# Routed experts of a mixture layer in three fp32r products instead of one fp32 product, with two output row buffers and another order of the weight loads

## The chip, the cores and the metric

The kernel runs on one core of a Trainium2 chip. The metric is the time of one execution on the device in microseconds, the median of several runs. A core has five engines with an instruction queue each: TensorE (PE; its weight loads are shown apart as PEld), VectorE (DVE), ScalarE (ACT), GpSimd (POOL) and SyncE (SP, which issues most DMAs). Engines wait for each other and for DMAs through semaphores only. Sixteen DMA engines move the data.

## What is computed

One layer of a transformer for 640 tokens of 1024 elements, with attention in two forms, and behind it a mixture of 64 small experts, of which each token takes eight. The part that the change touches is this:

```python
def swiglu(x, w1, w3, w2):
    return (jax.nn.silu(x @ w1) * (x @ w3)) @ w2

# tokens sorted by expert and padded to blocks of 128 rows; one expert a block
def run_block(args):
    xb, e = args
    return swiglu(xb, w_e1[e], w_e3[e], w_e2[e])      # 128x1024 @ 1024x256 (twice), 128x256 @ 256x1024
yd = lax.map(run_block, (xd.reshape(n_blocks, 128, d), blk_e)).reshape(n_rows, d)
return jax.ops.segment_sum(yd * wd[:, None], td, num_segments=t)
```

All is float32. A token goes to 8 experts, so there are 5120 rows, 80 to a block on average if every expert has one block; experts with more than 128 rows get a second block. With these inputs there are 70 blocks, the last six of them such second blocks with few rows.

## The kernel before

**The stages.** Modulation and norm, projections, two attentions, the merge and output projection (L1088 to L1217, which already works with rounded and remainder parts), router and shared expert, and then the loop over the routed blocks (L1685 to L1889), which takes from 1080 to 1905 us of the profiled execution. A last stage reads the sums back and adds the residual.

**The loop.** Every engine runs its own `step(n, i, u, guard)` for n = 0, 1, 2, ...; u is n modulo RING (4). `run` (L1688) unrolls the first four steps, runs the steps 4 to 63 in a loop of four, and then further fours with conditions on the number of blocks `nb`, which is only known at run time. `due` puts such a condition around a part. One step works on up to four blocks:

- GpSimd (L1744): `gather(n)` copies the block's row numbers and gathers its 128 rows from DRAM to `xg[n % 2]` by an indirect DMA (L1762), then `scatter(n-3)` (L1766) copies row numbers, waits for the scatter before (`s_sc`) and for the scaled output (`yV`, `yA`), and adds the rows of `yb` to the sums in DRAM with an indirect DMA that accumulates (L1777). Scatters of two blocks may hit the same token, so they run one at a time. `hold` (L1750) is a one-element instruction ahead of each.
- TensorE (L1788): `turn_x(n)` transposes the gathered rows (8 transposes, L1794), `down(n-2)` is the second layer (L1806: 4 products of 512 columns), `turn_g(n-1)` transposes the hidden rows (L1813), `up(n)` is the first layer with w1 and w3 side by side (L1821: 8 products of 512 columns). A float32 product is two MATMUL instructions in the profile.
- ScalarE (L1832): its half of `take_x(n)` (L1837, copy out of PSUM), its half of `take_y(n-2)` (L1845, scaled by the routing weight), `silu(n)` (L1853).
- VectorE (L1861): the other halves (L1866, L1873), `take_g(n-1)` (L1878), `product(n)` (L1882).
- SyncE (L1709): w1 and w3 of block n (`load_w13`, L1487, 2 x 1 MB, 8 KB to a partition each) once `up(n-4)` is done, then w2 (`load_w2`, L1491, 1 MB in rows of 4 KB) once `down(n-4)` is done. The weights of blocks 0 to 2 are loaded in the stage before.

There is one `yb`, so `take_y` of a block waits until the scatter of the block before has landed.

## Time and profile before

| | |
|---|---|
| median of 3 runs | 1926.02 us (1924.02 to 1927.55) |
| profiled execution, span | 1923.9 us |
| TensorE busy | 1775.5 us (92%) |
| VectorE, ScalarE, GpSimd busy | 574.9, 375.0, 430.1 us |
| granted TensorE clock, mean | 0.967 of full |
| data moved by DMA | 346 MB, 180 GB/s |
| loop over the routed blocks | 1080 to 1905 us |

Times in the rows are microseconds from the start of the span, or ns where a mean of one instruction is given. A busy time is what an engine worked; what stands after the bar or in brackets is how long it stood before, and for whom. Matmuls overlap in the pipeline: an instruction's own duration is longer than the distance from its start to the next one's, and the distance is what counts.

### The profile page before, as it was taken

Reading aid. Unit: us, or ns where it says so; the run is one execution under the profiler, and the core shown is the slowest. Engines: PE = TensorE matmul, PEld = TensorE weight load, DVE = VectorE, ACT = ScalarE, POOL = GpSimd, SP = SyncE. Lnnn points to the kernel's source line nnn. Section 1 sums busy time; section 2 is a strip of 40 time slices with the busy share of each in tenths; the row PEclk is TensorE's granted clock in tenths of the full one; section 3 lists DMA queues with packets and bytes.
Section 4 is the critical chain, followed back from the end, with each engine's and each line's share of the span. In section 5 each row is a group of like instructions: output and inputs, shape, how many; then the busy total and the mean of one; then the engine's idle time right before and its main releaser. Section 6 shows DMA issues by size and latency. Waiting matters only on the chain. (4 is left out here: it accounts for less than half of the span.)

```text
span 1923.9 us, 21816 instructions
## 1 busy us (share of the span) xinstructions
PE 1775.5 (92%) x7487; PEld 1077.7 (56%) x7487; DVE 574.9 (30%) x1221; ACT 375.0 (19%) x722; POOL 430.1 (22%) x630
## 2 busy tenths in 40 slices
PE   7979999869999799999985799999999999999993
PEld 2457767556666699996452344444444444444441
DVE  2444454454445500211661011121112121112213
ACT  3112222222323411220210111111111111111110
POOL 0010000020011233230016122333223333223321
PEclk9989999989999999999987899999999999999996
DMA  9311212200000332325250499999999999999953
GB/s 329 139 45 44 87 58 73 78 22 1 0 0 0 110 87 66 87 66 192 81 219 13 177 333 340 339 338 323 322 329 341 334 329 314 322 326 324 319 183 111
DMA packets 127327, 346.37 MB, mean 180 GB/s; under 512 B 20698, under 2 KB 60206, under 8 KB 109240
## 3 DMA queue, kind: packets, MB, share of 16 engines
q1 hardware_dynamic: 105130, 301.18, 42.2%
q0 software_dynamic: 21440, 42.08, 9.3%
q10 hardware_dynamic: 720, 2.62, 0.3%
q8 instruction: 22, 0.36, 0.1%
q14 instruction: 15, 0.12, 0.0%
HBM read 332.01 MB, written 45.25 MB: 196 GB/s over the span
## 5 line engine op out<-in xcount | busy, mean ns | idle before, releaser
L1821 PE MATMUL psum<-mem 128*128 128x512 f32 x1120 | 495.5, 595 | 1.1 <-DVE mem L1866 1.1
L1821 PEld LDWEIGHTS psum<-mem 128*128 128x128 f32 x1120 | 208.4, 191 | 238.0 <-issue 236.3
L1806 PE MATMUL psum<-mem 128*128 128x512 f32 x560 | 252.0, 593 | 1.4 <-DVE mem L1878 1.4
L1873 DVE TENSOR_SCALAR mem<-psum,mem 128x512 f32<-128x512 f32 x70 | 52.6, 751 | 442.8 <-DMA sums<-mem,si 431.5
L1806 PEld LDWEIGHTS psum<-mem 128*128 128x128 f32 x560 | 101.0, 190 | 102.5 <-issue 102.5
L1750 POOL TENSOR_TENSOR held<-nhalf 1x1 f32<-1x1 f32 x207 | 38.2, 184 | 482.5 <-DMA sums<-mem,si 406.8
L1845 ACT ACTIVATE mem<-psum,mem 128x512 f32<-128x512 f32 x70 | 48.1, 688 | 450.4 <-DMA sums<-mem,si 438.3
L1777 POOL DMA_INDIRECT sums<-mem,si x70 | 112.3, 1604 | 38.9 <-issue 38.9
L653 PE MATMUL psum<-mem 128*128 (+2 forms) x288 | 100.1, 448 | 9.3 <-ACT mem L764 7.1
L764 ACT ACTIVATE mem<-psum,small 128x640 f32<-128x640 f32 (+1 forms) x80 | 56.7, 709 | 243.4 <-DVE small L863 243.3
L863 DVE TENSOR_REDUCE small<-psum 128x1 f32<-128x640 f32 (+1 forms) x80 | 57.5, 718 | 134.4 <-PE psum L655 86.0
L1794 PEld LDWEIGHTS psum<-ident,mem 128*128 128x128 f32 x560 | 63.9, 142 | 54.7 <-issue 28.9
L1882 DVE TENSOR_TENSOR mem<-mem,psum 128x256 f32<-128x256 f32 x70 | 29.5, 422 | 205.1 <-ACT mem L1853 201.6
L1129 PE MATMUL psum<-h_hi,w_hi 128*128 128x320 f32 x256 | 80.4, 314 | 7.5 <-DVE h_lo L1196 7.5
L1794 PE MATMUL psum<-ident,mem 128*128 128x128 f32 x560 | 74.9, 277 | 11.2 <-PEq L1509 9.1
L1762 POOL DMA_INDIRECT mem<-h,gi x68 | 72.3, 1063 | 37.2 <-issue 37.2
L684 PE MATMUL psum<-mem 128*128 128x128 f32 x640 | 80.5, 275 | 0.0
L653 PEld LDWEIGHTS psum<-mem 128*128 128x128 f32 x288 | 46.3, 192 | 60.6 <-issue 49.2
L1130 PE MATMUL psum<-h_lo,w_hi 128*128 128x320 f32 x256 | 79.7, 311 | 0.0
L1131 PE MATMUL psum<-h_hi,w_lo 128*128 128x320 f32 x256 | 79.6, 311 | 0.0
L357 PE MATMUL psum<-mem,mem_h 128*128 (+1 forms) x640 | 77.7, 281 | 0.4 <-ACT mem L445 0.4
L357 PEld LDWEIGHTS psum<-mem,mem_h 128*128 128x128 f32 x640 | 75.9, 198 | 0.7 <-ACT mem L445 0.7
(249 smaller groups left out, 2470.5 us busy)
## 6 DMA issues: line engine op xcount, KB each, us to landing
mem<-in_w_e SPq DMA_DIRECT2D x210, 1024.0 KB, 7.8
mem<-in_w_mod SPq DMA_DIRECT2D x8, 2048.0 KB, 8.0
mem<-in_w_mod SPq DMA_DIRECT2D x8, 1024.0 KB, 12.2
mem<-in_x_sample SPq DMA_DIRECT2D x8, 512.0 KB, 11.2
mem<-in_w_in SPq DMA_DIRECT2D x1, 4096.0 KB, 15.2
wkvb<-in_w_in SPq DMA_DIRECT2D x8, 512.0 KB, 4.2
mem<-in_w_in SPq DMA_DIRECT2D x8, 512.0 KB, 4.3
mem<-in_w_out SPq DMA_DIRECT2D x1, 4096.0 KB, 16.4
```

The lines of the kernel that those rows point to most:

```text
L357: mm = pe.matmul(pZ[:, t * P:(t + 1) * P], hT[:, k, t * P:(t + 1) * P], wq[:, k, bass.ds(h * HD, HD)], start=(k == 0), stop=(k == KT - 1))
L653: mm = pe.matmul(pS[:, o:o + w], q, kT(c, w), start=True, stop=not mla)
L684: mm = pe.matmul(pO[:, (t - 1) * P:t * P], vh[:, kt, :], pT[:, j, (t - 1) * P:t * P], start=(j == 0), stop=(j == 4))
L863: dve.tensor_reduce(nmax[:, t:t + 1], pS[:, 0:w], AX_X, ALU.max, negate=True).then_inc(s["nm"], 1)
L1129: pe.matmul(out, whi[b][:, q, k, :], hi[:, k, cols_], start=(k == 0), stop=False)
L1130: pe.matmul(out, whi[b][:, q, k, :], lo[:, k, cols_], start=False, stop=False)
L1131: mm = pe.matmul(out, wlo[b][:, q, k, :], hi[:, k, cols_], start=False, stop=(k == KT - 1))
L1762: pool.indirect_dma_start(out=xg[u % 2], out_offset=None, in_=S["h2"], in_offset=bass.IndirectOffsetOnAxis(ap=gi[u % 2][:, 0:1], axis=0), ...
L1777: pool.indirect_dma_start(out=S["sums"], out_offset=bass.IndirectOffsetOnAxis(ap=si[:, 0:1], axis=0), in_=yb, in_offset=None, compute_op=A ...
L1794: tr = pe.transpose(pX[:, k * P:(k + 1) * P], xg[u % 2][:, k * P:(k + 1) * P], ident[:, :])
L1806: mm = pe.matmul(pY[:, c * 512:(c + 1) * 512], gT[:, f, :], w2[v][:, f, c * 512:(c + 1) * 512], start=(f == 0), stop=(f == 1))
L1821: mm = pe.matmul(pH.rearrange("p (a n) -> p a n", a=2), xT[:, k, :], w13[u][:, :, k, :], start=(k == 0), stop=(k == KT - 1))
```

## The change

Each product of the routed experts is made from parts: hi is the operand rounded to fp32r, lo is the remainder (also fp32r), and hi*hi + lo*hi + hi*lo are three matmuls in place of one in float32.

- `turn_x`, `turn_g` stay. `up` and `down` call `thrice`: 24 and 12 matmuls.
- ScalarE rounds: x (two copies out of PSUM, 512 columns each), w1 and w3 of the **next** block (2 copies of 2048 columns, behind `take_x`), w2 (one of 2048), g (256). It takes over the whole of `take_y` (1024 columns). The order of a step is take_x, next_w13, take_y, take_g, hi_w2, silu.
- VectorE subtracts: x (2 x 512), w1 and w3 of the next block (2 x 2048, in place in the ring buffer), g (256), half of w2 (1024). It no longer has a part of `take_y`. `product` writes g so that it matches the new order of w2's rows.
- GpSimd subtracts the other half of w2 (1024 columns), between its gather and its scatter.
- There are two `yb`; `take_y(m)` waits for the scatter of block m-2. The scatters still run one at a time.
- w2's partition p holds rows 2p and 2p+1 (8 KB in one piece) in place of p and 128+p.
- SyncE loads w13(n) and then w2(n-1); w2 waits for `down(n-5)`.
- The steps 60 to 63 move from the plain loop to the one with conditions.
- Before the loop ScalarE and VectorE make the parts of block 0's w1 and w3.

```diff
-    w2_src = I["w_e2"][0].rearrange("e (f p) n -> p e f n", p=P)
+    w2_src = I["w_e2"][0].rearrange("e (p f) n -> p e f n", p=P)
...
-    yb = mem.at(M_OB + 2560, D)
+    yb = [mem.at(M_H + 4096, D), mem.at(B0 + 2816, D)]
...
+                def lo_w2():
+
+                    v = (u - 2) % RING
+                    pool.wait_ge(se["h2"], n - 1)
+                    pool.tensor_tensor(wLo2[v][:, 1, :], w2[v][:, 1, :], wHi2[v % 2][:, 1, :].bitcast(F32),
+                                       ALU.subtract).then_inc(se["l2P"], 1)
...
                 due(pool, guard(0), gather)
+                due(pool, guard(2), lo_w2)
                 due(pool, guard(3), scatter)
...
+            def thrice(out, xh, xl, wh, wl, first, last):
+
+                pe.matmul(out, xh, wh, start=first, stop=False)
+                pe.matmul(out, xl, wh, start=False, stop=False)
+                return pe.matmul(out, xh, wl, start=False, stop=last)
...
-                    pe.wait_ge(s_w13[u], 32 * (i + 1))
+                    pe.wait_ge(se["xl"], 2 * n + 2)
+                    pe.wait_ge(se["l13"], 2 * n + 2)
                     for k in range(KT):
-                        mm = pe.matmul(pH.rearrange("p (a n) -> p a n", a=2), xT[:, k, :], w13[u][:, :, k, :],
-                                       start=(k == 0), stop=(k == KT - 1))
+                        mm = thrice(pH.rearrange("p (a n) -> p a n", a=2), xHi[:, k, :], xLo[:, k, :],
+                                    wHi13[u % 2][:, :, k, :], wLo13[u][:, :, k, :], k == 0, k == KT - 1)
...
+            def hi_w13(n, i, u):
+
+                act.wait_ge(s_w13[u], 32 * (i + 1))
+                for a in range(2):
+                    act.activation(wHi13[u % 2][:, a], w13[u][:, a], ACT.Copy).then_inc(se["h13"], 1)
...
+                    act.activation(yb[u % 2], pY, ACT.Copy, scale=wslot(tabs, m, 2).bitcast(F32)).then_inc(se["ye"], 1)
...
                 due(act, guard(0), take_x)
+                due(act, guard(-1), next_w13)
                 due(act, guard(2), take_y)
+                due(act, guard(1), take_g)
+                due(act, guard(0), hi_w2)
                 due(act, guard(0), silu)
...
+            def lo_w13(n, u):
+
+                for a in range(2):
+                    dve.wait_ge(se["h13"], 2 * n + a + 1)
+                    dve.tensor_tensor(wLo13[u][:, a], w13[u][:, a], wHi13[u % 2][:, a].bitcast(F32), ALU.subtract)                       .then_inc(se["l13"], 1)
...
                 due(dve, guard(0), take_x)
-                due(dve, guard(2), take_y)
+                due(dve, guard(-1), next_w13)
                 due(dve, guard(1), take_g)
+                due(dve, guard(0), lo_w2)
                 due(dve, guard(0), product)
```

## Rows read from the trace of the kernel before

**Rows 1.** Busy time by stretch: stretch, engines' busy time, clock, DMA share, GB/s.

```profile
1200.00:1300.00 100.00, 99.22 (x296) 47.62 (x295) 19.76 (x36) 15.03 (x27) 32.02 (x63) 1.00 0.98 341
...
1700.00:1800.00 100.00, 99.64 (x298) 48.20 (x297) 18.68 (x34) 14.18 (x26) 30.21 (x60) 1.00 0.90 316
```

**Rows 2.** One period in order of time: start, duration, instruction, idle before.

```profile
1400.10 1.61 POOL L1777 DMA_INDIRECT sums<-mem,si  x1 [0.56 <-issue]
...
1401.08 1.04 PE L1794 MATMUL psum<-ident,mem 128*128 128x128 f32 x8
...
1401.95 3.60 PE L1806 MATMUL psum<-mem 128*128 128x512 f32 x8
...
1402.69 1.06 POOL L1762 DMA_INDIRECT mem<-h,gi  x1 [0.51 <-issue]
1405.38 0.38 PE L1813 MATMUL psum<-ident,mem 128*128 128x128 f32 x2
...
1409.38 0.18 POOL L1750 TENSOR_TENSOR held<-nhalf 1x1 f32<-1x1 f32 x1 [5.63 <-DMA sums<-mem,si]
...
1411.07 1.61 POOL L1777 DMA_INDIRECT sums<-mem,si  x1 [0.56 <-issue]
...
1412.47 1.04 PE L1794 MATMUL psum<-ident,mem 128*128 128x128 f32 x8
```

**Rows 3.** Waits from 1200 to 1800 us: total, times, longest.

```profile
ACT mem L1845 <- DMA sums<-mem,si: 360.4, 52, 7.7
...
POOL held L1750 <- DMA sums<-mem,si: 318.2, 52, 7.0
```

**Rows 4.** Half microseconds of one period: as rows 1.

```profile
1405.50:1406.00 0.50, 0.50 (x4) 0.30 (x3) 0.00 (x0) 0.00 (x0) 0.00 (x0) 1.00 0.57 115
...
1412.50:1413.00 0.50, 0.50 (x6) 0.50 (x5) 0.00 (x0) 0.33 (x1) 0.41 (x3) 1.00 0.97 410
```

**Rows 5.** DMA, 1400 to 1500 us: rate by 2.5 us; packets, MB, share; gathers' landing.

```profile
GB/s 423 318 153 406 424 397 223 279 393 411 282 252 374 437 426 235 189 400 405 335 169 320 423 400 246 290 390 437 406 238 264 434 433 316 138 392 437 415 161 239
...
q0 software_dynamic: 2561, 5.97, 24.1%
...
DMA to landing us min/median/max: 7.0/9.0/10.4
```

**Rows 6.** The fp32r form in the merge stage, two starts that follow each other.

```profile
829.91 0.31 PE L1131 MATMUL psum<-h_hi,w_lo 128*128 128x320 f32 x1
...
830.06 0.31 PE L1129 MATMUL psum<-h_hi,w_hi 128*128 128x320 f32 x1
```

**Rows 7.** ScalarE's groups by form: busy, mean ns, idle before.

```profile
L1147 ACT ACTIVATE w_hi<-mem 128x1024 fp32r<-128x1024 f32 x16 | 16.0, 1050 | 68.5 <-DMA mem<-in_w_ob 34.5 <-DMA mem<-in_w_oa 34.0
...
L1151 ACT ACTIVATE oa_hi<-mem 128x640 fp32r<-128x640 f32 x8 | 5.1, 722 | 0.0
...
L1592 ACT ACTIVATE mem<-psum 128x1024 f32<-128x1024 f32 x5 | 5.1, 1024 | 28.5 <-PE psum L1539 16.3 <-remote 12.2
```

**Rows 8.** VectorE's groups by form, subtraction of 640 and a product of 1024 columns.

```profile
L1196 DVE TENSOR_TENSOR oa_lo<-mem,oa_hi 128x640 fp32r<-128x640 f32 x8 | 6.0, 812 | 0.0
...
L1918 DVE TENSOR_TENSOR mem<-mem 128x1024 f32<-128x1024 f32 x5 | 6.1, 1225 | 0.2
```

**Rows 9.** Subtractions of both engines side by side in the merge stage.

```profile
650.15 2.34 POOL L1186 TENSOR_TENSOR w_lo<-wkvb,w_hi 128x1024 fp32r<-128x1024 f32 x1 [26.29 <-ACT w_hi L1147]
...
662.07 6.57 POOL L1186 TENSOR_TENSOR w_lo<-mem,w_hi 128x1024 fp32r<-128x1024 f32 x1 [6.67 <-ACT w_hi L1147]
...
660.41 5.96 DVE L1196 TENSOR_TENSOR oa_lo<-mem,oa_hi 128x640 fp32r<-128x640 f32 x8
```

**Rows 10.** The loop's first products, and the clock in a stretch (as rows 1).

```profile
1080.13 1.94 PE L1794 MATMUL psum<-ident,mem 128*128 128x128 f32 x8 [9.09 <-PEq L1509]
...
1082.85 10.19 PE L1821 MATMUL psum<-mem 128*128 128x512 f32 x16 [0.78 <-DVE mem L1866]
...
1088.00:1089.00 1.00, 1.00 (x3) 0.35 (x2) 0.00 (x0) 0.00 (x0) 0.00 (x0) 0.50 1.06 434
```

More of the change, by code:

```diff
@@ L1740, in _ @@
                         n = RING * i + u
-                        step(n, i, u, lambda k, n=n: n < nb)
+                        with sp.If(n < nb):
+                            late(n, u)
         @block.gpsimd
@@ L1798, in down @@
                     v = (u - 2) % RING
[L1799 to L1800 removed]
+                    pe.wait_ge(se["gl"], n - 1)
+                    pe.wait_ge(se["l2V"], n - 1)
+                    pe.wait_ge(se["l2P"], n - 1)
                     if not (isinstance(n, int) and u == 2):
[L1802 to L1803 removed]
+                        pe.wait_ge(se["ye"], n - 2)
                     for c in range(2):
+                        cs = slice(c * 512, (c + 1) * 512)
                         for f in range(2):
[L1806 to L1807 removed]
+                            mm = thrice(pY[:, cs], gHi[:, f, :], gLo[:, f, :], wHi2[v % 2][:, f, cs], wLo2[v][:, f, cs],
+                                        f == 0, f == 1)
                     mm.then_inc(se["y"], 1)
@@ L1836, in take_x, with next_w13 @@
                     act.wait_ge(se["Tx"], n + 1)
-                    act.activation(xT[:, 4:8, :].rearrange("p k t -> p (k t)"), pX[:, 512:1024], ACT.Copy)\
-                       .then_inc(se["xeA"], 1)
+                    for h in range(2):
+                        act.activation(xHi[:, 4 * h:4 * h + 4, :].rearrange("p k t -> p (k t)"),
+                                       pX[:, 512 * h:512 * (h + 1)], ACT.Copy).then_inc(se["xh"], 1)
+                def next_w13():
+                    if not (isinstance(n, int) and n == 0):
+                        act.wait_ge(se["u"], n)
+                    hi_w13(n + 1, i + (u + 1) // RING, (u + 1) % RING)
                 def take_y():
@@ L1842, in take_y, with take_g, hi_w2 @@
                     act.wait_ge(se["y"], m + 1)
-                    if not (isinstance(n, int) and u == 2):
-                        act.wait_ge(s_sc, 16 * m)
-                    act.activation(yb[:, 512:1024], pY[:, 512:1024], ACT.Copy,
-                                   scale=wslot(tabs, m, 2).bitcast(F32)).then_inc(se["yA"], 1)
+                    if not (isinstance(n, int) and m < 2):
+                        act.wait_ge(s_sc, 16 * (m - 1))
+                    act.activation(yb[u % 2], pY, ACT.Copy, scale=wslot(tabs, m, 2).bitcast(F32)).then_inc(se["ye"], 1)
+                def take_g():
+                    act.wait_ge(se["Th"], n)
+                    if not (isinstance(n, int) and n < 2):
+                        act.wait_ge(se["y"], n - 1)
+                    act.activation(gHi[:, :, :].rearrange("p f t -> p (f t)"), pG[:, 0:256], ACT.Copy)                       .then_inc(se["gh"], 1)
+                def hi_w2():
+                    act.wait_ge(s_w2[u], 16 * (i + 1))
+                    if not (isinstance(n, int) and n < 2):
+                        act.wait_ge(se["y"], n - 1)
+                    act.activation(wHi2[u % 2][:, :, :], w2[u], ACT.Copy).then_inc(se["h2"], 1)
                 def silu():
@@ L1868, in take_y @@
-                def take_y():
-                    m = n - 2
-                    dve.wait_ge(se["y"], m + 1)
-                    if not (isinstance(n, int) and u == 2):
-                        dve.wait_ge(s_sc, 16 * m)
-                    dve.tensor_scalar(yb[:, 0:512], pY[:, 0:512], wslot(tabs, m, 2).bitcast(F32), None,
-                                      ALU.mult).then_inc(se["yV"], 1)
-                def take_g():
-                    dve.wait_ge(se["Th"], n)
-                    dve.tensor_copy(gT.rearrange("p f t -> p (f t)"), pG[:, 0:256]).then_inc(se["te"], 1)
+                    for h in range(2):
+                        dve.wait_ge(se["xh"], 2 * n + h + 1)
+                        dve.tensor_tensor(xLo[:, 4 * h:4 * h + 4, :].rearrange("p k t -> p (k t)"),
+                                          pX[:, 512 * h:512 * (h + 1)],
+                                          xHi[:, 4 * h:4 * h + 4, :].bitcast(F32).rearrange("p k t -> p (k t)"),
+                                          ALU.subtract).then_inc(se["xl"], 1)
```

96 lines of the change are left out of this document (55 added, 41 removed).

## Prediction

> **What bounds the kernel now.** I read the stretches first. From 1200 to 1800 us TensorE is busy for over 99% of every 100 us at full clock, while the DMA engines stand at 0.90 to 0.98 [rows 1]. That is the loop over the expert blocks, about 780 us of the 1924. Next I read one period in order of time [rows 2]: the eight transposes of a block start at 1401.08 and those of the next at 1412.47, so a block takes 11.4 us. It holds 8 second-layer and 16 first-layer matmul instructions of 0.43 us each (8 from 1401.95 to 5.38, 16 from 5.60 to 12.47), which is 10.3 us, and 1.1 us of transposes. The waits say that ScalarE and GpSimd do stand still, each over 300 us, for the scatter of the block before [rows 3], but TensorE does not wait for them.
>
> Two other things are nearly as slow. **The serial scatter**: started at 1400.10, landed at 1409.38, next one at 1411.07, so 11.0 us from one to the next. **The DMA engines**: from 1405.5 to 1406.0, with a scatter in flight, the share is 0.57 and the rate 115 GB/s, where it is 0.97 and 410 GB/s with weights alone [rows 4]. I read this as eight or nine of 16 engines busy and the others out of work. The Trainium skill ("DMA: Bandwidth & Descriptors", The descriptor swizzle) puts partitions 0 to 63 on eight engines, which the 0.57 fits. The queue rows give the load [rows 5]: 5.97 MB in 100 us (8.8 blocks) are 166 rows of 4 KB a block, so 83 gathered and 83 scattered, and 0.241 of 1600 engine-us over 729 such pairs is 0.53 us a pair. Eight pairs are 4.2 us; the weights, 3.15 MB at the 424 to 437 GB/s of the slices without a scatter, 7.3 us. A loaded engine thus has some 11.5 us of work in a period of 11.4: the sum is a touch high, and these engines have no slack.
>
> **The change, part by part.** TensorE: 12 products a block, each two passes of 0.43 us, become 36 of one pass. The same form ran with 320 columns at a start every 0.146 us [rows 6]; 512 columns at 2.4 GHz are 0.213 us, plus the 0.012 that 320 columns took over theirs, 0.226 us (scaled with the columns, 0.233). 36 x 0.226 + 1.1 = 9.2 us (9.5), so 2.2 us a block off TensorE.
>
> ScalarE gets most of the rounding. Copies of 640 and 1024 columns took 0.72 and 1.05 us, so 2048 take 1.93 [rows 7]. Its block: 3 x 1.93, take_x 2 x 0.60, take_y 1.02 + 0.09 for its scale, take_g and silu 0.39 each, in all 8.9 and with the gaps 9.2 us. Their order counts: take_y comes behind both w1/w3 roundings. VectorE: subtractions of 640 and 1024 columns took 0.81 and 1.23 us [rows 8], so 2.33 for 2048; 2 x 2.33 + 1.23 + 2 x 0.7 + 2 x 0.42 = 8.1 us (the strided product perhaps 0.3 more). GpSimd gets one subtraction of 1024 columns, 2.34 us alone, beside 4.1 us of its own in [rows 2].
>
> **VectorE and GpSimd stop each other.** In the stage that has this form, the GpSimd subtraction of 2.34 us took 6.57 when it started at 662.07 into a train of VectorE subtractions that ended at 666.37 [rows 9]. So it stands until the train is over and then runs in full. This agrees with the Trainium skill ("SBUF — State Buffer", SBUF: two separate sides): a pair of ports that is locked for the whole instruction, where VectorE has two SBUF inputs. By that rule the chain below stands as told; shared in proportion, the ports would let GpSimd's small instructions through and the scatter would start at T+6 to T+8.
>
> **The chain I expect.** Let T be the start of ScalarE's first w1/w3 rounding in a block. At T+3.9 both are done, at T+5.1 take_y. VectorE's two subtractions fill T+2.0 to T+6.65. GpSimd's subtraction, queued by then, goes to 9.0; VectorE's w2 half, waiting since 7.5, to 10.2; then GpSimd's hold, copy of the indices, hold and issue, 1.1 us as in [rows 2] (1409.38 to 1411.07 less the 0.6 us for take_y): the scatter starts at T+11.3. The gather behind it starts 2.6 us later (1400.10, 1402.69), lands after 8.0 us, and its transposes and take_x, which stand ahead of the rounding in ScalarE's order, take 1.1 and 1.25. This block is two ahead, so 2 P = 11.3 + 2.6 + 8.0 + 2.3 = 24.2, **P = 12.1 us**. The 8.0 is between the least and the median of now, 7.0 and 9.0 us [rows 5]: in a longer period the weights leave the queue empty for a while. With 7.0 P is 11.6, with 10.4 it is 13.3. If GpSimd's subtraction slips in before VectorE's pair instead, the scatter starts between T+7.7 and T+10 and P is 10.3 to 11.4 by this chain; but at a period below 11.8 each round ends some tenths later than the one before (scatter + 6.05 + 4.65 + 1.1 us is 11.8 after it), until the order turns over. So I take the late order, and keep the early one for the range.
>
> **The other edits.** The second output buffer takes 0.6 us from the scatter's chain (9.3 + 1.1 = 10.4 a block), under every other bound here. w1/w3 a block ahead of w2: the roundings need the weights two periods after their issue, and their transfer is 7.3 us; nothing, unless the DMA engines are the bound. 8 KB pieces: of a loaded engine's 7.3 us, a third in half as many packets; rows don't part the sizes; 0 to 0.15 us off, I take 0.1. Run-time conditions on four more blocks: nothing beside 11 us of work. **The ends**: the first product now waits for 2 x 1.93 us of rounding and a subtraction that itself stood behind one, so it starts near 1088 instead of 1082.85, but runs 7 to 8 us, not 9.6, as the clock is at half for part of it (1088 to 1089 still [rows 10]): +3. The first five blocks, before the chain is full, take about 10 us: -7. Six overflow blocks with few rows: -4. From the last first-layer product (1882.83) to the last scatter (1894.72) 11.9 us become 8: -4.
>
> **Sum.** 58 blocks x (12.1 - 11.4) = +41, less 12: +29. The profiled execution spans 1923.9 us and the median of the runs is 1926.0, 2.1 more; 1923.9 + 29 + 2.1 = **1955 us**. The bounds of the landing give 58 x 0.2 - 12 = 0 and 58 x 1.9 - 12 = +98.
>
> **Rivals.** (1) **The loaded DMA engines pace the loop** (0.33). For it: they have no slack now, and the chain is shorter if the early order holds. From about 1104 they have 60 blocks x 11.3, six of 7.3 with hardly a row, and 17 us of scatters of the first four: until 1843; 19 us of rounding, products, rounding of g and take_y on to the last scatter, 1862 instead of 1894.7: -33, **1893 us**. The gain is small as two blocks of it are only the lead that the buffers held. (2) **The rows spread evenly over the engines and the lock is loose** (0.07): 7.3 + 83/16 x 0.53 = 10.1 us by DMA, 9.6 by the chain (5.9 + 2.6 + 8.0 + 2.3, halved, is 9.4): 58 x -1.3 - 12 - 2 blocks of lead = -110, 1816. Against it: the share of 0.57. (3) **TensorE's clock falls** (0.10). It waits some 3 us a block for the gather where it waits for nothing now. Behind 9.1 us of idle the clock stood at 0.50 (1.2 GHz) and was still there from 1088 to 1089, after 8 us of work [rows 10]. If it falls in every second gap and the work after it loses 3 us, P is 13.6: +116, 2042. It counts only if the clock falls at all in such a gap, and no row of this loop shows one. (4) **The two meet** (0.05): P = 11.6, within 4 us of now. My forecast has 0.45. It is the side on which a faster TensorE is paid for by the chain scatter, gather, take_x, take_y; it decides from P = 11.6.
>
> Faster by over 0.2% (what a measurement of this kernel can tell): 0.33 + 0.07, and 0.03 of the forecast's low end: 0.43. Within: 0.06. Slower: 0.51. The range leaves out (2), most of (3) and the ends of the others: 1882 to 2000. The likeliest case alone is 1926 to 2000.
>
> **What would show it.** Transposes to transposes: 12.1 us (11.3 by the first rival, 10 by the second). GpSimd's w2 subtraction at 5 to 7 us instead of 2.4, starting under VectorE's pair. TensorE's transposes behind the gather, and DMA share under 0.93; by the first rival ScalarE's rounding waits for in_w_e and the share stays above 0.95. TensorE 9.2 us busy a block. I am wrong if ScalarE never waits for the gather's transposes, or if the scatter starts before T+8 throughout.

## The result and the profile after

The changed kernel takes 1986.5 us (median, 1985.5 to 1988.5) against 1925.7 for the kernel before in the same session: 1.032 times, 95% interval 1.030 to 1.033, so 60.8 us slower. The forecast was 29 us slower. Kernels are compared below by such ratios, since the kernel before took 1912 to 1924 us in the sessions of the experiments; 0.001 is 1.9 us. Periods read from profiles of different sessions carry that spread too, so differences of 0.2 us between them may be the session's.

The page of the changed kernel first: busy time by engine, then the rows of the 40 slices (1200 to 1800 us are slices 25 to 37).

```profile
PE 1701.1 (86%) x8327; PEld 1278.8 (64%) x8327; DVE 1035.4 (52%) x1431; ACT 829.8 (42%) x1072; POOL 728.0 (37%) x700
...
PE   7979999779999899999893888878788888887983
...
PEclk9989999989999899999886989998988888898996
DMA  9311222100000423225242988998888888888852
```

TensorE, over 99% busy before [rows 1], now has holes in nearly every slice of the loop, its clock is not full, and the DMA engines are less busy too. Nobody is at work all the time: a chain of waits sets the pace. The same stretches as in [rows 1]; the second row is the whole loop's middle:

```profile
1200.00:1300.00 100.00, 80.56 (x355) 64.62 (x353) 69.18 (x56) 64.04 (x62) 55.89 (x62) 0.91 0.92 315
...
1200.00:1800.00 600.00, 499.74 (x2193) 402.69 (x2192) 411.08 (x333) 390.28 (x381) 356.99 (x378) 0.91 0.87 301
```

The waits in these 600 us, which answer to [rows 3] (who waits, for whom, us in total, times, longest):

```profile
ACT e_xhi L1877 <- PE psum L1827: 145.6, 47, 7.3
...
PE psum L1827 <- DMA mem<-h,gi: 100.3, 31, 5.7
POOL held L1770 <- DMA sums<-mem,si: 97.2, 24, 5.7
POOL held L1770 <- DMA sums<-mem_h,si: 89.3, 23, 5.1
```

There are 47 scatters in the stretch. GpSimd waits for the landing of the last scatter ahead of all 47; TensorE waits for a gather 31 times. No engine waits for a result of VectorE in these 600 us: its subtractions can hold the chain up only by what they do to GpSimd. One and a half periods in order of time, which answer to [rows 2] (start, duration, instruction, idle before it):

```profile
1398.85 1.62 POOL L1803 DMA_INDIRECT sums<-mem,si  x1 [0.17 <-issue]
...
1401.11 3.71 ACT L1871 ACTIVATE e_whi<-mem 128x2048 fp32r<-128x2048 f32 x2
...
1401.45 1.06 POOL L1782 DMA_INDIRECT mem<-h,gi  x1 [0.51 <-issue]
...
1402.53 2.43 POOL L1790 TENSOR_TENSOR e_wlo<-mem,e_whi 128x1024 fp32r<-128x1024 f32 x1
...
1403.06 6.26 DVE L1929 TENSOR_TENSOR e_wlo<-mem,e_whi 128x2048 fp32r<-128x2048 f32 x2 [1.00 <-ACT e_whi L1871]
...
1410.57 0.27 POOL L1770 TENSOR_TENSOR held<-nhalf 1x1 f32<-1x1 f32 x1 [5.61 <-DMA sums<-mem,si]
...
1411.77 1.64 POOL L1803 DMA_INDIRECT sums<-mem_h,si  x1 [0.54 <-issue]
...
1414.26 1.97 PE L1827 MATMUL psum<-ident,mem 128*128 128x128 f32 x8 [5.56 <-DMA mem<-h,gi]
...
1417.23 3.72 ACT L1871 ACTIVATE e_whi<-mem 128x2048 fp32r<-128x2048 f32 x2
1419.18 4.49 DVE L1929 TENSOR_TENSOR e_wlo<-mem,e_whi 128x2048 fp32r<-128x2048 f32 x2 [1.00 <-ACT e_whi L1871]
...
1421.96 1.76 POOL L1770 TENSOR_TENSOR held<-nhalf 1x1 f32<-1x1 f32 x1 [4.08 <-DMA sums<-mem_h,si]
...
1424.66 2.13 POOL L1803 DMA_INDIRECT sums<-mem,si  x1 [0.55 <-issue]
```

Read GpSimd's lines alone. The scatter issued at 1398.85 is waited for until 1410.57, and the next one starts at 1411.77; that one is waited for until 1421.96. There GpSimd's operation on a single element, `hold`, takes 1.76 us instead of 0.18: it ends at 1423.72, just behind VectorE's second subtraction (1419.18 + 4.49 = 1423.67). I looked at the single instructions too: from 1200 to 1800 us 52 of these operations took over 0.3 us, and each of them ended 0.05 us after the end of a VectorE instruction, 36 behind the first that ended while they stood and 16 behind the second. All such operations of the stretch, in the kernel before and then in the changed one (ns min/median/max):

```profile
L1750 POOL TENSOR_TENSOR held<-nhalf x156: 184/184/187, 1201.5 to 1792.1; 1x1 f32<-1x1 f32 x156
```

```profile
L1770 POOL TENSOR_TENSOR held<-nhalf x141: 182/185/2128, 1209.4 to 1793.1; 1x1 f32<-1x1 f32 x141
```

I cut each period between two scatter starts, from the timeline of GpSimd from 1200 to 1800 us, into three parts: until the wait for the landing is over (**landing**), the first `hold` behind it (**hold**), and the way to the next scatter (**rest**). The means in us, with the ratio to the kernel before:

| kernel | period | landing | hold | rest | ratio |
|---|---|---|---|---|---|
| before | 11.51 | 9.81 | 0.18 | 1.51 | 1 |
| changed | 12.62 | 10.28 | 1.04 | 1.31 | 1.032 |
| y first | 11.98 | 9.78 | 0.65 | 1.55 | 1.014 |
| w2 remainder on VectorE | 12.96 | 10.89 | 0.83 | 1.25 | 1.046 |
| rows spread | 12.36 | 9.60 | 1.22 | 1.55 | 1.031 |
| gather first | 12.27 | 9.65 | 0.93 | 1.70 | 1.021 |
| short subtraction | 11.62 | 10.04 | 0.28 | 1.30 | 1.001 |
| subtraction in pieces | 12.01 | 9.82 | 0.61 | 1.58 | 1.019 |
| TensorE filled | 12.20 | 9.26 | 1.28 | 1.66 | 1.030 |
| y and gather first | 11.78 | 10.40 | 0.29 | 1.09 | 1.010 |
| w2 rows of 4 KB | 12.36 | 10.00 | 0.97 | 1.39 | 1.024 |
| one output buffer | 12.55 | 9.69 | 0.92 | 1.94 | 1.035 |
| before, rows spread | 11.39 | 9.67 | 0.18 | 1.54 | 0.997 |

With two arrays of sums nobody waits for the last landing, so the parts have no meaning: period 12.04, ratio 1.015; with both swaps too, 11.11 and 0.992.

Of the 1.1 us that a block got longer, 0.86 are the stretched `hold` and 0.47 the landing; the rest lost 0.2. The stretch can fall on the later operations too: the rest holds a second `hold`, which took 1.26 us at 1397.42.

### The profile page after: what moved, and what is told of

It is laid out like the page before. It is cut to its first block and busy times, and to the rows that moved or that the text cites. A ratio compares the mean times of both kernels' runs of the same rounds, so it can differ in the third digit from the quotient of the medians.

```text
span 1984.6 us, 24464 instructions
## 1 busy us (share of the span) xinstructions
PE 1701.1 (86%) x8327; PEld 1278.8 (64%) x8327; DVE 1035.4 (52%) x1431; ACT 829.8 (42%) x1072; POOL 728.0 (37%) x700
## 5 line engine op out<-in xcount | busy, mean ns | idle before, releaser
L1929 DVE TENSOR_TENSOR e_wlo<-mem,e_whi 128x2048 fp32r<-128x2048 f32 x140 | 374.6, 2715 | 83.1 <-ACT e_whi L1871 83.1
L1871 ACT ACTIVATE e_whi<-mem 128x2048 fp32r<-128x2048 f32 x140 | 260.3, 1916 | 8.1 <-PEq L1522 8.1
L1819 PE MATMUL psum<-e_whi,e_xhi 128*128 128x512 f32 x560 | 228.1, 407 | 7.8 <-DVE e_xlo L1935 7.8
L1820 PE MATMUL psum<-e_whi,e_xlo 128*128 128x512 f32 x560 | 222.0, 396 | 0.0
L1821 PE MATMUL psum<-e_wlo,e_xhi 128*128 128x512 f32 x560 | 221.9, 396 | 0.0
L1790 POOL TENSOR_TENSOR e_wlo<-mem,e_whi 128x1024 fp32r<-128x1024 f32 x70 | 173.6, 2481 | 8.7 <-ACT e_whi L1902 7.3
L1902 ACT ACTIVATE e_whi<-mem 128x2048 fp32r<-128x2048 f32 x70 | 135.4, 1934 | 0.0
L1819 PE MATMUL psum<-e_whi,e_ghi 128*128 128x512 f32 x280 | 133.3, 476 | 1.9 <-DVE e_glo L1945 1.9
L1820 PE MATMUL psum<-e_whi,e_glo 128*128 128x512 f32 x280 | 123.5, 441 | 0.0
L1821 PE MATMUL psum<-e_wlo,e_ghi 128*128 128x512 f32 x280 | 123.3, 440 | 0.0
L1820 PEld LDWEIGHTS psum<-e_whi,e_xlo 128*128 128x128 f32 x560 | 105.9, 189 | 22.3
```

What stands on the lines that cost most here:

```text
L1790: pool.tensor_tensor(wLo2[v][:, 1, :], w2[v][:, 1, :], wHi2[v % 2][:, 1, :].bitcast(F32), ALU.subtract).then_inc(se["l2P"], 1)
L1819: pe.matmul(out, xh, wh, start=first, stop=False)
L1820: pe.matmul(out, xl, wh, start=False, stop=False)
L1821: return pe.matmul(out, xh, wl, start=False, stop=last)
L1871: act.activation(wHi13[u % 2][:, a], w13[u][:, a], ACT.Copy).then_inc(se["h13"], 1)
L1902: act.activation(wHi2[u % 2][:, :, :], w2[u], ACT.Copy).then_inc(se["h2"], 1)
```

## Experiments: what holds the scatter up

**ScalarE takes y first.**

```diff
-                due(act, guard(-1), next_w13)
                 due(act, guard(2), take_y)
+                due(act, guard(-1), next_w13)
```

> The changed kernel with one swap: ScalarE takes y before it rounds the next block's w1/w3. My theory (a chain over two blocks: take_x, ScalarE's rounding, take_y, scatter, gather, transposes): take_y now ends 5.2 us after the start of the block's transposes (1.1 + 2.8 of products + 1.25) instead of some 8.3 or later, so the chain is (5.2 + 1.1 + 2.6 + 9.6) / 2 = 9.3 us a block and another bound takes over, the loaded DMA engines with 11.3 to 11.5 us: 1986 - 58 x 1.1 = about 1925 us. Rival (the loaded DMA engines or the clock of TensorE set the 12.57 us already): the order on ScalarE changes little, 1970 to 1990 us.

Measured: ratio 1.0142 (1.0125 to 1.0159), about 34 us less than the changed kernel, half of what I expected. The period is 11.98; taking y is off the path, but GpSimd still waits for the last landing in 92% of the periods. The rival's 1970 to 1990 us is out as well.

**The whole w2 remainder on VectorE.** GpSimd's subtraction is left out of the loop, VectorE's covers 2048 columns.

```diff
-                    dve.tensor_tensor(wLo2[u][:, 0, :], w2[u][:, 0, :], wHi2[u % 2][:, 0, :].bitcast(F32),
+                    dve.tensor_tensor(wLo2[u][:, :, :], w2[u], wHi2[u % 2][:, :, :].bitcast(F32),
```

> The changed kernel with the whole w2 remainder subtracted on VectorE (one instruction of 2048 columns), none on GpSimd. My theory: GpSimd's subtraction of 2.4 us and its waits under VectorE's pair leave the way to the scatter, which starts at T + 7.5 at the latest instead of between T + 7.4 and T + 10.7 (T is the start of ScalarE's first w1/w3 rounding); with the landing of 9.6 us the period is (7.5 + 2.6 + 9.6 + 2.3) / 2 = 11.0, under the DMA bound of 11.3 to 11.5: about 1925 us. VectorE has 9.3 us of work then, no bound. Rival (GpSimd's subtraction stands beside the path, the DMA engines or the clock set the period): 1975 to 1995 us.

Measured: 1.0464 (1.042 to 1.0508), 28 us **slower**; both theories missed. This was the run that turned me: if GpSimd's subtraction had been the link, this had to help. The scatter itself, in the changed kernel and then here, from 1200 to 1800 us (one of the two buffers each):

```profile
L1803 POOL DMA_INDIRECT sums<-mem_h,si x24: 1623/1628/2437, 1210.5 to 1791.2; - x24
```

```profile
L1796 POOL DMA_INDIRECT sums<-mem_h,si x23: 1607/3182/3445, 1212.8 to 1782.4; - x23
```

VectorE's longer train now falls on the instruction that issues the scatter, in every second block: the median is 3.2 us for the scatters out of this buffer and still 1.6 for those out of the other, the mean of all 2.4 instead of 1.8. The landing comes 0.6 us later. GpSimd waits longer for it than in the changed kernel, where these two rows had 89.3 and 97.2 us:

```profile
POOL held L1770 <- DMA sums<-mem_h,si: 151.9, 23, 7.5
POOL held L1770 <- DMA sums<-mem,si: 143.7, 23, 7.4
```

**The rows spread over the partitions.**

```diff
+            for at, by in ((32, 32), (64, -64), (96, 32)):
+                chain(dve.tensor_scalar(jv, posv, float(at), None, ALU.is_ge))
+                chain(dve.scalar_tensor_tensor(out=gsel, in0=jv, scalar=float(by * NBLK), in1=gsel,
+                                               op0=ALU.mult, op1=ALU.add))
```

> The changed kernel with the slots of a block laid out so that slots 32 to 63 stand in partitions 64 to 95 and slots 64 to 95 in partitions 32 to 63: with some 80 valid rows, 48 lie in partitions 0 to 63 and 32 above, instead of 64 and 16. If partitions 0 to 63 mean eight of the 16 DMA engines, a loaded one has 6 pairs instead of 8, 1.1 us less, and a gather lands some 1 to 2 us sooner. My theory: the landing stands once in the chain of two blocks, so 0.5 to 1 us a block: 1930 to 1957 us. Rival (the landing is the time behind the weights in the queues, whatever the rows' places): the landing stays at 9.6 us and the time within 5 us of 1986. If the DMA load is the bound: 58 x 1.1, 1922 us.

Measured: 1.0313 (1.0294 to 1.0333), no gain, though the median landing of a gather fell from 10.7 to 9.3 us (1200 to 1800 us) and the scatter's by 0.7. The hold and the rest grew by 0.4 in exchange: what lands sooner meets VectorE's train instead. Over 58 blocks the period by scatter starts is 12.30 against 12.57, 16 us in all, but the first scatter came 8 us late (1117.8 against 1109.4). My theory missed the time. The rival had the time, within 5 us, but not its reason: the landing does depend on where the rows stand, and the time hardly on the landing alone. The same edit in the kernel before:

> The kernel BEFORE with the rows spread. The prediction says that TensorE bounds it (over 99% busy) and that scatter and DMA engines are only nearly as slow: then the shorter landing buys nothing and the operations ahead of the loop cost some 8 us: ratio 1.002 to 1.006. If the serial scatter or the loaded engines bound the kernel before already, its period of 11.5 us falls by 0.3 to 1.0: ratio 0.974 to 0.995.

Measured: 0.9973 (0.9963 to 0.9984), and in the middle of the loop

```profile
1200.00:1800.00 600.00, 600.00 (x1794) 1.00 0.93 331
```

TensorE is busy for all 600 us; it was 597.89 with the rows as they were. So **the kernel before was bound by TensorE**, but for 0.1 us a block. A late gather is part of that: TensorE waited for one five times in the 600 us, 1.6 us in all, and not once here. Where the rest of the 5 us gained comes from is open. The eight us that the first scatter came late in the run above did not show here (1105.9 against 1107.8), so they are not the price of the six operations.

**The gather ahead of the scatter on GpSimd**, that of the next block.

```diff
-                due(pool, guard(0), gather)
                 due(pool, guard(2), lo_w2)
+                due(pool, guard(-1), gather)
                 due(pool, guard(3), scatter)
```

> The changed kernel with one swap on GpSimd: the gather of the next block is issued ahead of the scatter and behind the w2 subtraction, no longer behind the scatter. My theory: the gather starts near T + 10.5 instead of T + 13.3, so the period by this chain is (9.0 + 1.5 + 9.6 + 2.3) / 2 = 11.2 us, under the DMA bound of 11.3 to 11.5: about 1925 us. Rival (what holds the gather back is not the scatter ahead of it on GpSimd but the DMA queues, so it lands when the engines have served the weights): the landing grows by what the start gains, 1975 to 1990 us.

Measured: 1.021 (1.0193 to 1.0227), 21 us less, a third of what I expected. The scatter still waits for the last landing in 73% of the periods.

**VectorE's w1/w3 subtraction short.**

```diff
-                    dve.tensor_tensor(wLo13[u][:, a], w13[u][:, a], wHi13[u % 2][:, a].bitcast(F32), ALU.subtract)
+                    dve.tensor_tensor(wLo13[u][:, a, 0], w13[u][:, a, 0], wHi13[u % 2][:, a, 0].bitcast(F32), ALU.subtract)
```

> The changed kernel with VectorE's two w1/w3 subtractions cut from 2048 to 256 columns each (seven eighths of the remainder of w1/w3 is left out; TensorE multiplies by the rounded part there, so its 36 products, the transfers and the work of ScalarE and GpSimd stay as they are). My theory after the first four runs: the scatters run one at a time, and behind a scatter's last data GpSimd cannot go on before VectorE's train of subtractions is over; the time from a scatter's last data packet to the next scatter is 4.5 us on average, against 2.3 in the kernel before with 0.6 of it for taking y. Without the long subtractions some 2.8 us of it go, the DMA load takes over at 11.3 us a block: 1986 - 58 x 1.2 = 1905 to 1920 us. Rival (the landing of the gather, or TensorE's half clock in the gaps, sets the period): 1970 to 1990 us.

The edit has a second half that is not shown: TensorE multiplies by the rounded part where the remainder is left out. Measured: 1.001 (0.9991 to 1.0028), the whole loss gone, with TensorE's 36 products, ScalarE's rounding, GpSimd's subtraction and every transfer in place. The hold is at 0.28 us on average instead of 1.04, the landing 0.24 shorter: 58 x 1.0 is 58 of the 59 us gained. This is the main evidence that the loss comes from VectorE's long subtractions. The run alone does not part what they do to GpSimd from the later start of VectorE's own next steps; the waits of the changed kernel do, as nobody waits for VectorE there.

**The same subtraction in four pieces each.**

```diff
+                    for k in range(0, KT, 2):
+                        op = dve.tensor_tensor(wLo13[u][:, a, k:k + 2], w13[u][:, a, k:k + 2],
+                                               wHi13[u % 2][:, a, k:k + 2].bitcast(F32), ALU.subtract)
```

> The changed kernel with each of VectorE's two w1/w3 subtractions of 2048 columns cut into four of 512, back to back. If VectorE keeps GpSimd out for as long as its train of two-input instructions goes on without a gap (as the prediction read it), the time stays: 1980 to 1996 us (six more instructions of some 0.05 us overhead). If GpSimd gets its turn at the end of each instruction, its small operations slip in and the stall behind a scatter's landing falls from some 2.8 to 0.5 us: 1910 to 1930 us.

Measured: 1.0189 (1.0161 to 1.0216), 25 us less, between the two theories; mean hold 0.61. One hold of this run and the VectorE train above it:

```profile
1415.38 0.70 POOL L1770 TENSOR_TENSOR held<-nhalf 1x1 f32<-1x1 f32 x1 [4.12 <-DMA sums<-mem_h,si]
...
1410.02 6.02 DVE L1930 TENSOR_TENSOR e_wlo<-mem,e_whi 128x512 fp32r<-128x512 f32 x8 [1.00 <-ACT e_whi L1871]
```

The train ends at 1416.04, the hold at 1416.08. That is the wait for one piece: the last of the eight, 0.68 us long, had started at 1415.36, just before the hold. Another case, in the middle of a train from 1436.50 to 1441.41:

```profile
1439.15 0.49 POOL L1770 TENSOR_TENSOR held<-nhalf 1x1 f32<-1x1 f32 x1 [2.76 <-DMA sums<-mem_h,si]
1439.60 0.65 POOL L1798 COPY si<-mem 128x1 int32 x1
1440.32 0.53 POOL L1770 TENSOR_TENSOR held<-nhalf 1x1 f32<-1x1 f32 x1
```

GpSimd gets its turn at the end of a piece, and its next small operation stands behind a piece again: three operations of 0.2 us took 1.7 us. Of the 81 holds over 0.3 us, 52 ended behind the first VectorE instruction that ended in them, 27 behind the second and 2 behind the third; why some miss the first end is open. So GpSimd waits for single instructions, mostly, and not for the whole train.

**TensorE kept at work.**

```diff
+                    for _ in range(3):
+                        pe.matmul(bank(6), ident[:, :], x1[:, 0, 0:512], start=True, stop=True)
```

> The changed kernel with three more fp32 matmuls of 512 columns (0.86 us each) behind each block's first-layer products, into a PSUM bank that nobody reads: TensorE is at work while it would wait for the gather, so that its clock stays at 2.4 GHz. Rival (TensorE's clock, at half after a gap in about every third block, carries the loss: transposes 2.0 us instead of 1.0, second-layer products 5 instead of 2.8): the period falls by 0.7 to 1 us, 1930 to 1945 us. My theory (the scatter's landing and the lock carry it, TensorE's slow stretches lie mostly beside): within 12 us of 1986, whatever the granted clock does.

Measured: 1.0296 (1.0276 to 1.0316), 4 us less, within the 12 us of my theory. The clock is full throughout:

```profile
1200.00:1800.00 600.00, 595.43 (x2560) 436.22 (x2558) 452.87 (x346) 400.35 (x394) 404.86 (x395) 1.00 0.90 311
```

**This does not price the clock.** The row shows TensorE busy for 595.43 of 600 us, and it waits for a gather for 4.4 us only: with the filler it is itself a bound. From transposes to transposes it takes 12.1 us, of which the filler has 2.6:

```profile
1410.17 1.09 PE L1827 MATMUL psum<-ident,mem 128*128 128x128 f32 x8
...
1419.70 2.74 PE L1858 MATMUL psum<-mem,ident 128*128 128x512 f32 x6
1422.27 1.04 PE L1827 MATMUL psum<-ident,mem 128*128 128x128 f32 x8
```

Even so the 58 blocks in the middle were 12.16 us apart by their scatters instead of 12.57, 24 us in all. Most of that is lost at the ends, where the fifth scatter starts 6.5 us later and the last seven gaps are 5.8 us longer; and the kernel before was 4 us faster in that session, which the ratio takes off. So the half clock may carry some 0.4 us of the 1.04 that a block got longer, or more; the filler also moves TensorE's steps, and no run parts the two. That the clock is not all of it is shown elsewhere: with two arrays of sums (below) the period falls by 0.5 us with the clock at 0.92, where it was 0.91.

**Both swaps.**

> The changed kernel with both swaps of the first runs: y is taken before the roundings on ScalarE, and the gather is issued ahead of the scatter on GpSimd. Alone they gave -35 and -23 us. If they shorten the same chain (scatter, landing, next scatter) by moving GpSimd's work out of VectorE's train, the second gives little on top: 1940 to 1955 us. If they shorten two different chains (the first the scatter's, the second the gather's), they add up to the DMA bound of 11.3 to 11.5 us: 1920 to 1930 us.

Measured: 1.0095 (1.0078 to 1.0111). Alone they gave 1.75% and 1.07%, together 2.2%: they mostly shorten the same thing, as the first theory has it (1944 us by the ratio, in its range). The hold is down to 0.29: GpSimd seldom waits under the train any more. The serial landing, 10.4 us, is what is left.

## Experiments: the serial scatter itself

**Two arrays of sums.** Blocks scatter in turn into two arrays, each with its own semaphore and list of indices; the second is zeroed ahead and added at the end. The first eight steps are unrolled instead of four.

```diff
-                        pool.wait_ge(s_sc, 16 * m)
+                        pool.wait_ge(s_sc[(u - 3) % 2], 16 * (2 * i + (u - 3) // 2))
...
-                    pool.indirect_dma_start(out=S["sums"], out_offset=bass.IndirectOffsetOnAxis(ap=si[:, 0:1], axis=0),
+                    pool.indirect_dma_start(out=S[("sums", "sums2")[(u - 3) % 2]], out_offset=bass.IndirectOffsetOnAxis(ap=si[(u - 3) % 2][:, 0:1], axis=0),
```

> The changed kernel with two arrays of sums in DRAM: even blocks scatter into the one, odd blocks into the other (zeroed beforehand, added at the end), so that a scatter waits for the landing of the one before the last, not of the last. My theory by now: the period of 12.6 us is the serial scatter: 10.3 us from a scatter's start until the wait for its landing is over, 1.0 us for GpSimd's first small operation, stretched under VectorE's train, and 1.3 us to the next scatter. With two arrays the period falls to the chain over the gather or the load of the DMA engines, 11.3 to 11.9 us: 1986 - 58 x 1.0 + 5 for the longer end, 1920 to 1950 us. Rival (the gather's landing sets the pace and the scatter only follows it): 1980 to 1996 us.

Measured: 1.0149 (1.0117 to 1.0181), 32 us less. By the ratio that is 1954 us, a little above my theory's 1920 to 1950, and the rival is out. The period is 12.04 us, and GpSimd waits no more for a landing; TensorE still waits for gathers, 86.7 us in 31 periods. So the changed kernel has **two chains close together**: the scatter's at 12.6 and, once it is gone, the gather's at 12.0. They share GpSimd's way to the scatter, so a hold that is stretched lengthens both.

**The same with both swaps.**

> The same two arrays of sums, in the kernel with both swaps (y before the roundings on ScalarE, the gather ahead of the scatter on GpSimd), which had a period of 11.85 us, 10.4 of it from a scatter's start to the end of the wait for its landing. My theory: that serial wait is what is left, so the loaded DMA engines take over at 11.3 us or a little below: 1941 - 58 x 0.5 + 5, 1905 to 1925 us, level with the kernel before or faster. Rival (the DMA engines set the 11.85 already): 1938 to 1950 us.

Measured: **0.9917 (0.9899 to 0.9935)**, 1910 us by the ratio, in my theory's range and faster than the kernel before. Each edit alone gave 1.7 to 2.2%, both 4.0%. From 1200 to 1800 us:

```profile
1200.00:1800.00 600.00, 538.50 (x2486) 417.17 (x2485) 510.21 (x379) 446.23 (x433) 396.34 (x433) 1.00 0.95 337
```

The clock is full without any filler, and the period is 11.11 us.

**w2 in 4 KB rows again.**

```diff
-    w2_src = I["w_e2"][0].rearrange("e (p f) n -> p e f n", p=P)
+    w2_src = I["w_e2"][0].rearrange("e (f p) n -> p e f n", p=P)
```

> The changed kernel with the w2 rows in 4 KB pieces again (and VectorE's product back to contiguous columns). Question: why does a scatter take 10.3 us to land where it took 9.8 before? One theory: its rows take turns with the weights' packets, and a packet of 8 KB holds an engine for 0.34 us where one of 4 KB holds it for 0.18; with a third of the bytes in short packets again the landing falls by 0.4 to 0.5 us, the period with it: 1955 to 1965 us. The other theory (the landing is longer for the other place of the scatter between the transfers, not for the packets' size): 1980 to 1992 us, as the prediction put the size of the pieces at 0 to 0.15 us a block.

Measured: 1.0237 (1.0213 to 1.0261), 15 us less. Undoing both, the 8 KB pieces and the strided product, gains 0.3 us a block where the prediction gave the 8 KB pieces a gain of 0.1. The scatter's landing falls by 0.3 us, less than the first theory's 0.4 to 0.5, and the median landing of a gather by 0.9 (10.7 to 9.8). By the ratio the time would be 1971 us beside the changed kernel's 1986, between the two forecasts. The contiguous product is in the same edit, so its part isn't split off. In the kernel whose scatter nobody waits for:

> The kernel with two arrays of sums and both swaps (0.992 of the kernel before, a block in 11.1 us, no wait for a scatter's landing left), with the w2 rows in 4 KB pieces and contiguous columns in the product. In the changed kernel that undoing was worth 0.3 us a block. If the gain came through the scatter's landing (10.3 to 10.0 us), which nobody waits for here, the ratio stays at 0.988 to 0.995. If the loaded DMA engines themselves get their work done sooner with short packets, it repeats: 58 x 0.3 us, 0.983.

Measured: 0.9929 (0.991 to 0.9949), no different from 0.9917. That fits a gain through the landings, which nobody waits for here; it does not say which of the two, the scatter's or the gather's.

**One output buffer.**

```diff
-                        act.wait_ge(s_sc, 16 * (m - 1))
+                        act.wait_ge(s_sc, 16 * m)
```

> The changed kernel with one output row buffer instead of two: ScalarE may take y only when the last scatter has landed. The prediction gave the second buffer 0.6 us of the scatter's chain, under every other bound, so 1986 to 1990 us without it by that reading. If the serial scatter sets the period, as I think by now, taking y (1.1 us, and ScalarE's w2 rounding, take_g and the next roundings behind that wait) comes on top of it: 58 x 1.1 to 58 x 3, 2050 to 2160 us.

Measured: 1.0348 (1.0329 to 1.0367), 6 us slower; my 58 us and more was wrong. Taking y behind the landing (rest 1.94 instead of 1.31) only takes the place of a landing 0.6 us shorter. By the ratios the second buffer is worth 0.1 us a block, and the two intervals touch; 0.1 us is too little to be read from the periods.

## Experiments: what bounds the fastest kernel

> The kernel with two arrays of sums and both swaps, with the rows spread (slots 32 to 63 and 64 to 95 of a block exchange partitions, 48 of 80 rows in the lower half instead of 64). If the loaded DMA engines set its period of 11.1 us, as the prediction's account has it (7.3 + 8 x 0.53 = 11.5), six pairs instead of eight take 1.1 us off that bound; TensorE's 9.5 and ScalarE's 9.2 us are next, so P is 10.1 to 10.5: 58 x 0.8 = 46 us less, plus some 8 us for the six more operations ahead of the loop: ratio 0.970 to 0.978. If another chain sets the 11.1 us, only the 8 us remain: 0.992 to 0.998.

Measured: 0.9922 (0.9905 to 0.994), period 11.09. The load of the eight engines is not the bound.

> Both edits of the two runs before it together: the candidate for the fastest. If both take work off the same engines, the sum of their gains; if the rows' spread alone makes the landing short enough, the time of the spread kernel alone, within 3 us.

Measured: 0.9918 (0.99 to 0.9935), period 11.07: the same again. Then the hold-up between the two w2 subtractions:

> The kernel with two arrays of sums and both swaps (period 11.1 us, nobody waits for a DMA), with the whole w2 remainder on VectorE, none on GpSimd. In its trace GpSimd's subtraction (2.80 us) and VectorE's half (3.08 us instead of 1.21) hold each other up, and VectorE's product, transposes of g and remainder of x come behind them: TensorE waits 0.5 us for the one and 0.7 us for the other in each block. If that sets the 11.1 us, one subtraction of 2.3 us in place of the two frees VectorE at 3.1 - 2.3 + 0.9 = up to 1.6 us sooner, and the period falls by 0.5 to 1.1 us: ratio 0.957 to 0.977. If the loaded DMA engines set it after all (7.3 + 8 x 0.53, which the estimate had at 11.5), it stays: 0.988 to 0.995. The same edit in the changed kernel, where the serial scatter waits behind VectorE's train, made it slower by 1.5%.

> The kernel of the run before it with the rows spread over the partitions as well (48 of 80 rows in the lower half instead of 64). If the loaded DMA engines are the bound that it meets once GpSimd's subtraction is gone, the spread takes up to 58 x 0.5 us more off: a ratio lower by 0.01 or more than that of the run before. If TensorE (9.5 us and its waits) is the bound, the same within 0.004.

Measured: 0.9914 (0.9892 to 0.9936) and 0.9898 (0.9877 to 0.992), periods 11.18 and 11.07: neither gain came. The first lies where the expectation had it for the loaded DMA engines; the second rules these out, as its rows are spread. The timeline of TensorE in the first of them says why:

```profile
1423.74 1.04 PE L1821 MATMUL psum<-ident,mem 128*128 128x128 f32 x8
1425.31 0.49 PE L1813 MATMUL psum<-e_whi,e_ghi 128*128 128x512 f32 x1 [0.53 <-DVE e_glo L1938]
...
1428.18 0.38 PE L1840 MATMUL psum<-ident,mem 128*128 128x128 f32 x2
1429.07 0.50 PE L1813 MATMUL psum<-e_whi,e_xhi 128*128 128x512 f32 x1 [0.51 <-DVE e_xlo L1928]
...
1434.53 0.39 PE L1815 MATMUL psum<-e_wlo,e_xhi 128*128 128x512 f32 x1
1434.76 1.04 PE L1821 MATMUL psum<-ident,mem 128*128 128x128 f32 x8
```

From transposes to transposes 11.0 us, of which TensorE stands still 0.53 for the remainder of g and 0.51 for that of x. Each wait costs more than that, as the steps around it no longer overlap: the product behind the transposes of x starts 0.79 us after them where nothing is waited for (0.87 in [rows 2]), and here their whole 1.04 us and the wait pass first, likewise 0.38 instead of some 0.14 for those of g. The run with the filler has the work without waits: 12.1 us less six instructions in 2.57 us is **9.5 us of work a block**. So the two remainders that VectorE takes between steps of TensorE cost 1.5 us together. In the kernel before that work was 11.4 us without a wait. The subtraction moved, and with it which remainder is late, but not the sum. This bound would need TensorE's steps in another order; that wasn't tried.

## Why the prediction was right in sign and wrong in size

**Before is bound by TensorE: right.** The kernel before with the rows spread has TensorE busy 600.00 of 600 us.

**The failed step is the scatter's chain**, "9.3 + 1.1 = 10.4 a block, under every other bound here". It was 12.6 and set the pace. Its terms: the landing was read from one period of [rows 2], 9.28 us, and is 9.81 on average in the kernel before; it became 10.28. The 1.1 us behind it became 1.04 + 1.31, since the first of GpSimd's small operations stands behind VectorE's instructions. The prediction had the rule for this at hand and laid it on GpSimd's subtraction alone, the largest operation, and not on the two in the middle of the serial chain, `hold` and the issue of the scatter. The short subtraction takes the loss away (1.001), two arrays of sums take away 32 us of it.

**The gather's chain: right in sum, by two errors that cancel.** The forecast was 11.3 + 2.6 + 8.0 + 2.3 = 24.2 for two blocks. The means of the changed kernel from 1200 to 1800 us are 8.9 from ScalarE's rounding to the scatter, 2.8 to the gather, 11.1 to its transposes, 2.4 to the next rounding: 25.2. The scatter comes 2.4 us sooner (1401.11 to 1411.77 is 10.7 us, 1417.23 to 1424.66 is 7.4). I took the late order throughout; in both of these periods GpSimd's subtraction starts ahead of VectorE's pair (1402.53 against 1403.06, 1415.49 against 1419.18), and what the scatter waits for is the last landing; the gather takes 3.1 longer, its median landing being 10.7 us where I took 8.0 between bounds of 7.0 and 10.4. I took the low side because the queues would be empty at times. With the scatter's chain out of the way the period is 12.04, against the 12.1 of the forecast. That agreement is luck: the parts are not those of the forecast there either, with a gather still landing after 10.5 us in the median.

**The account of the time.** The prediction took 58 x (12.1 - 11.4) = 41 us for the loop and 12 us off at the ends. From the scatter starts, the loop gave 58 x (12.57 - 11.53) = 60. At the ends the first scatter is 1.6 us later and the four gaps behind it 2.7 longer, as the scatter's chain is full from the first block on; the last seven gaps are 4.6 us shorter: together nothing. The forecast had -4 us where +4.3 came (start and first five blocks) and -8 where -4.6 came (overflow blocks and end), so the 12 us off at the ends is **the second step that failed**. 19 us of the loop and 12 of the ends are the difference of 31 to 32.

**Who holds up whom.** I expected GpSimd's subtraction at 5 to 7 us under VectorE's pair. It took 2.42 (at most 2.45 from 1200 to 1800 us, 4.1 in the whole loop), since it mostly starts first; VectorE's, with a median of 2.29, took up to 5.1 instead. So the rule of the Trainium skill that I cited ("SBUF — State Buffer", SBUF: two separate sides) holds in both directions here, 1.76 us for an operation of 0.18 and 6.26 for a pair of 4.5, and it lies on every link of GpSimd's that has an operation, however small. My reading of [rows 9], that GpSimd stands until the train is over, went too far for this loop: most of its stretched operations ended behind the VectorE instruction under way.

**8 KB pieces**: forecast -0.1 us, measured +0.3 with the strided product, through a landing. **Second buffer**: under another bound, as said, 0.1 us. **TensorE's work**: forecast 9.2 us (9.5 with the starts scaled with the columns), 9.5 in the run with the filler: a product of 512 columns starts every 0.233 us, the scaled value. It decided nothing in the changed kernel; with the two remainders on its way it is the bound of the fastest. **ScalarE and VectorE**: 1.92 us for 2048 columns (1.93 forecast), 2.29 (2.33); the strided product took 0.60 instead of 0.42 us.

**The rivals.** (1) The loaded DMA engines as a bound of 11.3 us: no. Three kernels with the same load ran at 11.1, and spreading the rows left them there. Why 7.3 + 8 x 0.53 is too high was not tried; packets that overlap in part would explain it. That the loaded half lengthens the landings is what the spread rows show. (2) The spread of rows: it isn't even, as the shorter landings show. (3) The clock does fall, to 0.91 on average, and its share in the loss is open: with it at full 4 us come back in all, but 24 in the middle of the loop, in a run whose filler made TensorE a bound. The rival's sum (13.6 us a block) did not come. (4) did not occur.

## What to carry to other kernels

In a serial chain, price every operation on every engine of it, the tiny ones too, with what the change puts beside them; an operation on one element can stand until an instruction of the other engine ends, and the next one again. Read a link's duration as the mean over the stage and not from one period, and take for the new kernel a landing no shorter than the old one unless a row shows it. When chains lie close together, removing one shows only the distance to the next: from 12.6 us to 12.0 with the serial scatter gone, to 11.8 with GpSimd mostly out of VectorE's train, and to 11.1, the bound of TensorE and the remainders that it waits for, only with both. And look at what a probe adds before you read its total: the filler that kept the clock up became a bound itself.

## What the runs showed of the hardware that I had not expected

- VectorE's train of two-input subtractions stretched GpSimd's operation on one element from 0.18 to as much as 2.13 us and the instruction that issues an indirect scatter from 1.6 to as much as 3.4 us. The stretched one-element operations ended 0.05 us after the end of a VectorE instruction, mostly the one under way; cut into instructions of 0.68 us, the subtractions held several of GpSimd's operations in a row for one piece each.
- TensorE's clock fell to half (1.2 GHz) behind an idle stretch that began at 1408.70, was at half when the products came back, and rose some 4.5 us after them (stretch, us, busy, clock, DMA share, GB/s):

```profile
1411.00:1412.00 1.00, 0.00 (x0) 0.96 0.87 352
...
1413.00:1414.00 1.00, 0.00 (x0) 0.50 0.99 414
1414.00:1415.00 1.00, 0.74 (x4) 0.50 1.03 434
...
1419.00:1420.00 1.00, 1.00 (x6) 1.00 0.51 152
```

- With w2 in 8 KB rows instead of 4 KB (and a strided product, in the same edit) the scatter landed 0.3 us later on average and the gather 0.9 in the median, and placing 48 instead of 64 of some 80 rows in partitions 0 to 63 made a gather land 1.4 us sooner.
